# Conditioning rows in column groups, and the recurrence's four chunks of a tile at once

## What is computed

```python
ada = silu(c) @ w_ada + b_ada              # 9 conditioning vectors -> shift1, scale1, gate1, shift2, scale2, gate2
h = rms(x) * gain * (1 + scale1) + shift1
q, f, i, g, u = split(h @ w_in)            # 5 x 512 columns
o_h = hgrn2(q, 1 - f, i, log f, state)     # 4 heads; in chunks of 32 tokens:
#   o     = (masked scores) v + (q exp(cum)) state
#   state = exp(last) * state + (k exp(last - cum))^T v
o_s = s5(u, state_ssm)                     # state space layer, then GLU and norm
x += gate1 * (concat(o_h, o_s) @ w_out)
x += gate2 * hier_moe(norm(x))             # 32 experts, two for each token
y = norm(x) * (1 + scale_f) + shift_f      # scale_f, shift_f = silu(c) @ w_ada_final + b_ada_final
```

## Time and profile before

| | |
|---|---|
| three runs | 1019.76, 1031.27, 1036.3 us (median 1031.27) |
| the profiled execution, its own time | 1016.35 us |
| its span (first to last instruction) | 1014.6 us |
| busy: PE, DVE, ACT, POOL | 794.4, 352.7, 208.3, 87.1 us |
| share of the chain that ended last: PE, issue, DMA, DVE, ACT's queue | 69, 7, 7, 6, 5 % |
| mean granted TensorE clock | 0.872 |

### The profile page before, as it was taken

One profiled execution on the slowest core, in us unless ns is written; L12 is line 12 of the kernel. 1 busy time (PEld: TensorE's weight loads), 2 busy tenths in 40 slices (PEclk: granted clock), 3 DMA queues, 4 the chain that ended last, 5 costly groups with the idle time before them and its releaser, 6 DMA issues.

```text
span 1014.6 us, 8295 instructions
## 1 busy us (share of the span) xinstructions
PE 794.4 (78%) x3102; PEld 381.3 (38%) x3102; DVE 352.7 (35%) x904; ACT 208.3 (21%) x445; POOL 87.1 (9%) x134
## 2 busy tenths in 40 slices
PE   6188999999997999897769999905866788787900
PEld 1025566563353442776434442302322333233300
DVE  2029374554753234235424542330100101010157
ACT  2032122424325434101011111201100101010122
POOL 1000100111100000100000000041100101110040
PEclk9687999999998999559779999956977989898955
DMA  7941112015341004500187407462989999999562
GB/s 264 343 136 55 44 40 83 1 63 187 103 171 64 22 20 165 126 1 11 42 305 258 116 31 254 183 165 78 373 348 416 391 396 413 395 399 406 227 195 93
DMA packets 62850, 187.33 MB, mean 185 GB/s; under 512 B 12475, under 2 KB 17723, under 8 KB 50518
## 3 DMA queue, kind: packets, MB, share of 16 engines
q1 hardware_dynamic: 39542, 154.46, 40.4%
q10 hardware_dynamic: 16256, 17.04, 5.7%
q0 software_dynamic: 7008, 15.25, 4.7%
HBM read 176.84 MB, written 17.22 MB: 191 GB/s over the span
## 4 chain that ended last, share of the span: by engine, by line
PE 69%; issue 7%; DMA 7%; DVE 6%; ACTq 5%; ACT 3%; POOL 1%; POOLq 0%; SPq 0%; DVEq 0%
PE ps L1538 64%; DMA sb<-in_moe_w_up 4%; DVE sb L937 3%; PE ps L1590 3%; ACTq L618 2%; ACTq L612 1%; PE ps L1685 1%; POOL token_of_row L512 1%; ACT sb L713 1%; DVE sb L1519 1%; DVE sb L1531 1%; DMA token_of_row<-sb 1%; DMA sb<-in_b_ada_final 1%; DMA sb<-y_rows,sb 1%; DMA out_hgrn_sample<-sb 0%
## 5 line engine op out<-in xcount | busy, mean ns | idle before, releaser
L1538 PE MATMUL ps<-sb 128*64 128x512 f32 (+10 forms) x2718 | 741.5, 502 | 105.4 <-issue 51.8
L1538 PEld LDWEIGHTS ps<-sb 128*128 128x128 f32 (+4 forms) x2718 | 333.3, 168 | 480.9 <-issue 416.7
L937 DVE TENSOR_TENSOR sb<-sb 128x16 f32<-128x16 f32 (+17 forms) x367 | 163.0, 485 | 101.8 <-ACT sb L713 47.9
L937 DVE TENSOR_TENSOR sb<-ps,sb 128x256 f32<-128x256 f32 (+6 forms) x69 | 28.9, 440 | 237.3 <-ACT sb L890 188.8
L1590 PE MATMUL ps<-sb 128*128 128x128 f32 (+1 forms) x208 | 31.6, 303 | 36.6 <-DMA sb<-h_rows,sb 33.0
L1590 PEld LDWEIGHTS ps<-sb 128*128 128x128 f32 (+1 forms) x208 | 27.2, 197 | 53.6 <-DMA sb<-h_rows,sb 33.1
L890 ACT ACTIVATE sb<-ps 128x256 f32<-128x256 f32 x16 | 6.2, 385 | 177.3 <-PE ps L1538 177.3
L520 POOL DMA_INDIRECT sb<-h_rows,sb x16 | 16.3, 1017 | 157.3 <-PE ps L1590 154.9
L713 ACT COPY sb<-ps 32x144 f32<-32x144 f32 x64 | 26.2, 410 | 11.1 <-PE ps L1538 9.6
L660 ACT ACTIVATE sb<-ps 128x512 f32<-128x512 f32 x12 | 7.2, 597 | 101.7 <-PE ps L1538 101.7
L1244 DVE SCALAR_TENSOR_TENSOR sb<-sb,ps 128x128 f32<-128x128 f32 x60 | 16.8, 342 | 31.5 <-PE ps L1538 31.5
(11 more groups left out here) (229 smaller groups left out, 347.6 us busy)
## 6 DMA issues: line engine op xcount, KB each, us to landing
sb<-in_moe_w_gate SPq DMA_DIRECT2D x32, 1024.0 KB, 13.5
...
```

The lines of the kernel that those rows point to most:

```text
L937: return dve.tensor_tensor(out, x0, x1, op)
L1538: return pe.matmul(out, lhsT, rhs, start=start, stop=stop, skip_group_check=True)
```

## The change

1. **Start.** Pieces 0 to 3 are now row blocks of w_ada (256 rows by 2048 columns, runs of 8 KB), each used for all four half rows at once: cT is padded to 32 columns, and half row (v, h) goes to the 32 partitions of quadrant(v, h), so that four consecutive products lie in four column groups (first_rows). One copy by ACT and four transposes (ada_cols) take the place of four copies, 16 transposes and two copies. The order of a weight matrix's rows in SBUF changes from (p c) to (c p). SP issues x ahead of the pieces. The 15 loads of L612 to L624 move from ACT to POOL. PE turns tiles 0 and 1 of x ahead of the rows.
2. **Later rows.** Both halves of a vector are made together, alternating between two column groups (rows_into). beside_s5 holds vectors 2, 3, 4 at its places 4, 5, 6 and nothing at 7; vector 5 stands in the preparation; 6 and 7 around the router. Rows are stored to DRAM by halves: 24 transfers where there were 12.
3. **Recurrence.** chunk_sums(t) makes the sums of a tile's four chunks at once, each chunk from its own 32 rows (row group) and into its own bank (U_BANK); carry(t) is DVE's four state steps; from_states(t) makes the queries of all four chunks, each in its own column group; seven state buffers. Tile t's queries stand behind tile t+1's sums, and tile t-1's norm and transposes behind that. The sample tile does all eight sequences at once, in two groups, with one instruction for each sequence and head in DVE, and its output transfers stand behind ACT's last copy.

```diff
-        pieces = [ada_cols(v, h) for v, h in ADA]
+        pieces = [w_ada[2 * P * n:2 * P * (n + 1), 0:2 * D].rearrange("(c p) n -> p c n", p=P) for n in range(4)]
...
+        def quadrant(v, h):
+            return 32 * (2 * (v % 2) + h)
...
-            eng.dma_start(ada_dram[v], rows8[q:q + 1, v // 4, :]).then_inc(done, 16)
+            for h in range(2):
+                q, ns = quadrant(v, h), slice(512 * h, 512 * h + 512)
+                eng.dma_start(ada_dram[v][:, ns], rows8[q:q + 1, v // 2, :]).then_inc(done, 16)
+                eng.dma_start(ada_tok[v][:, :, ns], rows8[q + 1:q + C9, v // 2, :].unsqueeze(1).to_broadcast([NB, TS, 512]))\
+                    .then_inc(done, 16)
...
+            for t in range(TILES):
+                src = a["x_prompt"][0, t * P:(t + 1) * P, :] if t < PT else a["x_sample"].rearrange("b t d -> (b t) d")
+                sp.dma_start(xin[0:ROWS[t], t, :], src).then_inc(S["x_in"], 16)
             for n in range(N0):
-                if n == 1:
-                    sp.wait_ge(S["prm_in"], 16 * 10)
                 if n >= 4:
                     sp.wait_ge(*used_up(n - 4))
...
-                if n == 1:
-                    for t in range(TILES):
-                        src = a["x_prompt"][0, t * P:(t + 1) * P, :] if t < PT else a["x_sample"].rearrange("b t d -> (b t) d")
-                        sp.dma_start(xin[0:ROWS[t], t, :], src).then_inc(S["x_in"], 16)
...
+            for k, name in enumerate(("ssm_b_re", "ssm_b_im")):
+                pool.dma_start(bin_[k], a[name][0].rearrange("g p h -> (g p) h").rearrange("(r q) h -> q r h", q=P))\
+                   .then_inc(S["bc_in"], 16)
...
+            pool.dma_start(ghg, a["hgrn_norm"].to_broadcast([P, DH])).then_inc(S["small_in"], 16)
...
+            def first_rows():
+                act.copy(rows8[:, 0, :], ada_wait()[:, :]).then_inc(S["ada_out"], 1)
...
-            for k, name in enumerate(("ssm_b_re", "ssm_b_im")):
-                act.dma_start(bin_[k], a[name][0].rearrange("g p h -> (g p) h").rearrange("(r q) h -> q r h", q=P))\
-                   .then_inc(S["bc_in"], 16)
...
-            for v, h in ADA:
-                ada_row(v, h)
-                if (v, h) == ADA[0]:
-                    act.wait_ge(S["x_in"], 16 * TILES)
-                    act.wait_ge(S["ss_init"], 1)
...
-            ada_col(0)
-            ada_col(1)
...
+            act.wait_ge(S["ms"], 1)
+            act.activation(rs[:, 0:TILES], ss[:, 0:TILES], ACT.Sqrt).then_inc(S["rms"], 1)
+            first_rows()
+            ada_cols()
...
-                    for w in ADA_HGRN:
-                        ada_row(*w)
+                    ada_rows(5)
...
-                    for half in range(2):
-                        act.wait_ge(S["s0_new"], half + 1)
-                        act.dma_start(o["hgrn_sample"][0, 4 * half:4 * half + 4].rearrange("b h k v -> k (b h) v"),
-                                      S0[half].rearrange("k b h v -> k (b h) v")).then_inc(S["s0_out"], 16)
...
+                if t >= 1:
+                    copy_mix(t - 1)
+            copy_mix(PT)
+            act.wait_ge(S["s0_new"], H)
+            for half in range(2):
+                act.dma_start(o["hgrn_sample"][0, 4 * half:4 * half + 4].rearrange("b h k v -> k (b h) v"),
+                              S0[half].rearrange("k b h v -> k (b h) v")).then_inc(S["s0_out"], 16)
...
-            mask(0)
-            for t in range(PT):
+            def carry(t):
+
+                dve.wait_ge(S["u_mm"], t + 1)
                 for j in range(4):
                     c = 4 * t + j
-                    dve.wait_ge(S["u_mm"], c + 1)
-                    new, old, U = Sr[(c + 1) % 3], Sr[c % 3], ps[6 + c % 2].rearrange("p (h v) -> p h v", h=H)
+                    new, old, U = Sr[(c + 1) % 7], Sr[c % 7], ps[U_BANK[j]].rearrange("p (h v) -> p h v", h=H)
                     if c == 0:
                         ins = dve.tensor_copy(new, U)
                     else:
+                        if j == 2 and t >= 1:
+                            dve.wait_ge(S["o_mm"], t)
                         dve.wait_ge(S["s_upd"], c)
                         for h in range(H):
...
                     ins.then_inc(S["s_upd"], 1)
-                if t + 1 < PT:
-                    mask(t + 1)
-                norm_o(t)
-            mask(PT)
-            for half in range(2):
...
+            for t in range(PT):
+                carry(t)
+                mask(t + 1)
+                if t >= 1:
+                    norm_o(t - 1)
+            dve.wait_ge(S["o_mm"], PT)
+            for b in range(4):
+                ins = dve.tensor_scalar(Vm[0:NS, b, :], V[0:NS, PT, :], seqm[:, b:b + 1], None, ALU.mult)
+            ins.then_inc(S["vm_ready"], 1)
+            norm_o(PT - 1)
+            dve.wait_ge(S["s0_in"], 32)
+            dve.wait_ge(S["o_mm"], TILES)
+            for h in range(H):
+                dve.wait_ge(S["us_mm"], h + 1)
+                for g in range(2):
+                    for b in range(4):
+                        U = ps[U_BANK[2 * (h % 2) + g]][:, P * b:P * (b + 1)]
+                        ins = dve.scalar_tensor_tensor(out=S0[g][:, b, h, :], in0=S0[g][:, b, h, :],
+                                                       scalar=dls[:, h, 4 * g + b:4 * g + b + 1], in1=U, op0=ALU.mult, op1=ALU.add)
                 ins.then_inc(S["s0_new"], 1)
...
+            def first_rows():
                 bank = ada_bank()
-                w = next_piece()
-                q = 32 * (v % 4)
+                for n in range(4):
+                    w = next_piece().rearrange("p c n -> p (c n)").rearrange("p (c n) -> p c n", c=2)
+                    for c in range(2):
+                        for q in range(4):
+                            ins = mm(bank[32 * q:32 * q + 32, :], cT[:, 2 * n + c, :], w[:, c, 512 * q:512 * q + 512],
+                                     n == 0 and c == 0, False)
+                    ins.then_inc(S["ada_part"], 1)
+                for q in range(4):
+                    ins = add_bias(bank, q // 2, q % 2)
+                ins.then_inc(S["ada_mm"], 1)
+            def rows_into(bank, v):
+                w = [next_piece() for _ in range(2)]
                 for c in range(KC):
-                    ins = mm(bank[q:q + C9, :], cT[:, c, :], w[:, c, :], c == 0, False)
-                j = 2 * v + h
+                    for h in range(2):
+                        q = quadrant(v, h)
+                        mm(bank[q:q + 32, :], cT[:, c, :], w[h][:, c, :], c == 0, False)
+                for h in range(2):
+                    ins = add_bias(bank, v, h)
+                ins.then_inc(S["ada_mm"], 1)
...
-            for v, h in ADA[:3]:
-                ada_row(v, h)
+                turn_tile(t, xin[:, t, :], (ps[2 + 2 * (t % 2)], ps[3 + 2 * (t % 2)]), S["tr_h"], True)
-            ada_row(*ADA[3])
-            ada_col(0)
-            ada_col(1)
+            first_rows()
+            ada_cols()
...
-            beside = [(4, 5), (6, 7), (8, 9), (10, 11), ADA_S5[0:2], ADA_S5[2:3], ADA_S5[3:5], ADA_S5[5:6]]
+            beside = [(4, 5), (6, 7), (8, 9), (10, 11), (2,), (3,), (4,), ()]
...
+            def chunk_sums(t):
+
+                if t:
+                    pe.wait_ge(S["s_upd"], 4 * t)
+                for h in range(H):
+                    hs = slice(P * h, P * (h + 1))
+                    for j in range(4):
+                        js = slice(CH * j, CH * (j + 1))
+                        ins = mm(ps[U_BANK[j]][:, hs], KhT[js, t, hs], V[js, t, hs], True, True)
+                ins.then_inc(S["u_mm"], 1)
+
+            def inside(t):
...
+            def from_states(t):
+
+                for h in range(H):
+                    for j in range(0 if t else 1, 4):
+                        js = slice(CH * j, CH * (j + 1))
+                        ins = mm(ps[4 + t % 2][js, P * h:P * (h + 1)], qT[:, h, t * P + CH * j:t * P + CH * (j + 1)],
+                                 Sr[(4 * t + j) % 7][:, h, :], False, True)
+                ins.then_inc(S["o_mm"], 1)
...
+            scores(0)
+            pe.wait_ge(S["ada_out"], 8)
+            chunk_sums(0)
+            for t in range(PT):
+                inside(t)
+                scores(t + 1)
+                if t + 1 < PT:
+                    chunk_sums(t + 1)
+                else:
+                    pe.wait_ge(S["s_upd"], NCH)
+                from_states(t)
+                if t >= 1:
+                    turn_mix(t - 1)
...
+            for h in range(H):
+                for b in range(4):
+                    for g in range(2):
+                        gs = slice(32 * g, 32 * g + 32)
+                        ins = mm(ps[4 + PT % 2][gs, P * h:P * (h + 1)], QhM[:, h, b, gs], S0[g][:, b, h, :], False, True)
+            ins.then_inc(S["o_mm"], 1)
+            for h in range(H):
+                if h >= 2:
+                    pe.wait_ge(S["s0_new"], h - 1)
+                for g in range(2):
```

(11 more changed lines are left out.)

283 lines of the change are left out of this document (116 added, 167 removed).

## The result

The changed kernel takes 911.28 us (median of four runs, 905.98 to 915.73) where the kernel before took 1029.37 in the same job (1019.76 to 1036.3): a ratio of 0.888, 95% interval 0.878 to 0.898. Runs that were clearly slower than the fastest of the same kernel are left out of the ratios, so a ratio is not exactly that of the two medians. The forecast was 920 in a range of 888 to 955. The profiled execution took 915.73 with a span of 914.0, so 100.6 us less than the 1014.6 of before. These two executions understate the change: the medians are 118.1 apart, since the profiled execution of before (1016.35) was quicker than all four of its runs here and that of after is the slowest of its four. The table accounts for the 100.6; where the other 17.5 lie is not shown.

What follows compares the result with a forecast made beforehand. The experts were taken as bound by their weights, the stages ahead by PE working slowly or waiting. Terms summed to -102.5: 914 us for a profiled execution, moved to a forecast of 920, range 888 to 955.

Steps and rivals of the forecast that it cites:

- The bound: Experts from 695 us: bound by their weights, 270 us long whenever they begin, so time won before comes through.
- Start: From kernel start to the projections: these begin at 48.5 in place of 84.32 us, -36 us.
- The tail behind the rows: Start, between the last row products with their bias and the projections: 10.5 us in place of 11.96.
- S5: S5 stage: six half rows become three pairs, but the chain through DVE and ACT limits the gain to -9 us.
- The chain argument: S5 rounds 2 and 3: the 34.85 us chain from PE's T through DVE limits each gain to 4.5 us.
- Preparation: Head 3 of the preparation: two half rows become one pair, PE is the bound, -7.8 us.
- Recurrence: Recurrence stage: 66 us in place of 108.5, with a tile's period of 10.5 us, -42 us.
- GLU: GLU's first part: PE idles about 10.5 us as sample-state outputs land behind ACT's last copy, +7.5 us.
- Late rows: Vectors 6 and 7 around the router: pairs save 7.8 us and another 7 to 8, -15 us.
- POOL's transfers: Loads moved from ACT to POOL: end at 42 to near 50 us, before DVE needs them at 64, 0 us.
- The rival of late loads: POOL's small loads, at 16 ns for each piece, end 34 us late, giving 945 us; chance 0.12.
- the slower kernel: S5 waits for POOL's costly descriptors, giving 1047 us at 32 ns each; chance of this side 0.02, of slower 0.01.

Runs made afterwards that it cites:

- The square of four kernels: Small loads on ACT or POOL: kernel before 1027.88 us on ACT, 1014.22 on POOL; changed kernel 928.83 on ACT, 911.28 on POOL.

## Why the prediction was right, point by point

The time was 9 us below the forecast and inside its own range; the sum of the terms, -102.5, met -106.4 up to the experts and -100.6 in all. That is closer than the terms deserve, and luck: the recurrence gave 18 more than I said, the start and S5 gave 5 and 7 less, the experts took 5.8 more, and these cancel. The 9 us come from the last step: for a profiled execution the sum says 914 and 915.73 was measured, then I added 6 for the medians, and the median came out 4.5 below the profiled execution.

- **The bound.** Time won ahead of 695 us came through but for 5.8 us. From the experts' first transposes to the last write of their rows it took 270.7 us before and 276.5 after, but 272.7 and 275.6 in two more executions of the same changed kernel, and 276.1 in the kernel before with only the loads moved. The 5.8 are of the size by which this stage differs from run to run; the claim "as long whenever it begins" stands.
- **Start, -36 forecast, -31.1 measured.** The tail behind the rows (43.0 to 53.25, 10.3 us for 10.5) was right. The squares came 2 us later than forecast (17.57), and the first transposes ended at 30.1 and not at 27; neither counted, as PE then waited for the last piece all the same. The mis-sized step is the landing of that piece: 33 forecast, 38.4 measured. I divided 10.75 MB by a steady stretch's 360 GB/s from 3 us on and put nothing beside it; POOL's loads ran beside it, and with them back on ACT the piece landed at 33.2.
- **S5, -9 forecast, -2.0 measured.** The chain argument held to half a microsecond: -4.4 and -4.3, with PE waiting 3.49 ahead of each T. What failed is the sentence "so rounds 2 and 3 each give at most 4.5, and PE idles for the rest": I put no price on the idle. The stage from T of round 3 on grew by 6.7 us, most of it in Y, which took 12.2 us at the low clock for 6.0. With the place filled the clock did stay up, and 4.1 came back.
- **Preparation, -7.8 forecast, -7.0 measured.** Right, with two column groups as the reason: undone, 5.2 of it went.
- **Recurrence, -42 forecast, -60.2 measured**, outside my bounds of 57 to 91 for its length: 48.2. The step that failed is "a tile now costs its sums and then DVE's carry". The period was 6.87 and not 10.5 (10.9 us over three), and it is the carry of 4.66 with 2.2 of DVE's mask and norm, which I had left out; the sums lie beside these. Their price was wrong too: I took the mean of two clocks, and 4.0 at the high one from a row that mixes several shapes, where even in one row group after another they cost 2.75, and 1.10 in four. Two further steps were mis-sized. The sample tile and its ends took 19.7 us from the last carry on and not 25 (queries of the last tile and Vm 2.6 and not 5). The first carry ended at 7.9 and not 9.4. Row groups account for 2 to 4 of the 18, by the clock of the stretch, column groups in the queries for less than 1.
- **GLU, +7.5 forecast, +8.5 measured**, an idle of 11.2 for 10.5: right, and shown by taking the transfer away from ACT (an idle of 3.5).
- **Late rows, -15 forecast, -14.6 measured**, half ahead of the logits (-7.9 in the pair of vector 6) and half by DVE's wait (8.69 to 0.90): right.
- **POOL's transfers, 0**: right for the S5 stage, for a reason I did not have, and wrong for the start, where they cost the 5 us named above. The rival of late loads (and with it the slower kernel) fell by a wide margin: POOL issued all within 10.1 us (4.41 to 14.47), at 0.6 to 1.4 us each, and they landed 10 to 15 us after their issue, all by 30 and not at 42 to 50. The sentence that put the rival's price at 8 to 32 ns a run took POOL to pay for each run apart; 560 packets for 0.94 MB, and 10.1 us for some 5,800 runs, do not fit that. The Trainium skill, "DMA: Bandwidth & Descriptors", section "Issuing engine by pattern", calls the other path generally faster than GpSimd's; for the issuing of these loads the measurement is the other way round (11.57 us of ACT's list for a load that POOL issues in 1.19), and it decides here.
- **The start's causes.** The theory for the loads put back on ACT laid the whole of its gain to ACT's list. The square of four kernels shows that the list alone is worth 13.4 us, the rows with the order of x and of the transposes 13.7, and both together 31.1.
